# A block with product-key experts: 64 more tokens get their gates by accumulating transfers instead of one-hot matmuls

## The chip, the cores and the metric

The kernel runs on one core of a Trainium2 chip. The metric is the device time of one execution in microseconds (us). TensorE (PE) does the matmuls, VectorE (DVE) and ScalarE (ACT) the elementwise work, GpSimd (POOL) issues the indexed transfers, SyncE (SP) the plain ones.

## The reference

Two transformer layers follow each other; each ends in an expert layer ("peer"). Only the expert layer matters here. For 256 tokens, 8 heads and two halves per head, 128 scores are computed; the best 16 of each half are taken, their 256 sums are formed, the best 16 sums are taken, and each names one of 128 x 128 experts:

```python
top_s, top_i = lax.top_k(s, PEER_TOPK)
cand_s = top_s[..., 0, :, None] + top_s[..., 1, None, :]
cand_i = top_i[..., 0, :, None] * PEER_NKEYS + top_i[..., 1, None, :]
best_s, best_pos = lax.top_k(cand_s.reshape(...), PEER_TOPK)
idx = jnp.take_along_axis(cand_i.reshape(...), best_pos, axis=-1)
gate = jax.nn.softmax(best_s, axis=-1)
act = jax.nn.gelu(jnp.einsum('bpd,bphkd->bphk', hb, u))
out = jnp.einsum('bphk,bphkd->bpd', act * gb, v_tab[ib])
```

So each token has 8 x 16 = 128 picks, each an expert and a gate.

## The kernel before

The kernel doesn't gather experts. It computes all 16,384 experts for all 256 tokens: activations in `arena` (expert row i on the free axis, 128 columns per partition), then multiplies them by a matrix of gates that is zero where an expert was not picked, and then multiplies by the second table. An expert layer b (1 or 2) has these stages, in order of time:

1. `wq` and scores: the queries, and the 16 x 128 scores of each token in `s_area`.
2. u stage: 128 units of the first table, each 512 KB, stream through `ring` (four slots). ACT rounds a half unit (L1390), DVE takes the rest (L1393), PE does 24 matmuls a unit (L1315 to L1317), ACT takes the gelu (L1414). Between two half units DVE does one slot of other work, by the function `between`: in `topk_part` the ranking of one head of 128 tokens (10 slots), in `lookup_part` the finding of the experts and gates of 4 such items (18 slots). The slots are counted: 4 rounds of 4 items and one lookup make 4 x 58 = 232 slots of the 256 half units. Rounds 0 and 1 are the 8 heads of tokens 0 to 127, rounds 2 and 3 those of tokens 128 to 255.
3. Gates of tokens 0 to 127: after lookups 0 and 1 (`picks_ready`), POOL issues in `pool_scatter` 128 indexed transfers a layer (L1532), one for each head and rank. Each adds 128 words, one for each token, to a matrix in DRAM, `gates_dram`, that SP has filled with zeros early in the kernel (`zero_part`, 32 transfers in all, L1546). Two transfers may name the same cell, so the 16 transfers of a head wait until those of all heads before have landed (semaphore `scattered`).
4. Gates of tokens 128 to 255: PE turns the picks (`pe_turn`), then a one-hot stage makes 16 groups (`NG`) of 8 tokens: DVE and ACT write one-hot rows (`dve_hots` L1559 to L1564, `act_hots` L1573 and L1577), PE multiplies them (L1589), DVE multiplies the activations by the result (`dve_multiply`, L1598).
5. v stage: 128 units of the second table. SP first waits for `scattered` of the whole layer, then loads the gate rows from DRAM into `gring` (L1782), four ahead. DVE multiplies tokens 0 to 127 of an expert row by them (`multiply`, L1608), ACT and DVE split the product and the table (L1630, L1631, L1635, L1638), PE accumulates the output in all eight banks (L1321, L1322).

POOL does nothing else in the whole kernel.

Of the kernel before, what the change touches and what calls it, by code (L numbers as in the profile page):

```python
# [56 lines left out]
ZEROS = 512  # L57
NPROJ = 3
# [99 lines left out]
CONSTS = [("ident", 128), ("blk64", 128), ("iota", 128), ("token", 64)]  # L158
# [37 lines left out]
def shape_constants():  # L196

    i = np.arange(P)
    f32 = np.float32
    common = {  # L200
        "ident": np.eye(P), "blk64": i[:, None] // 64 == i[None, :] // 64,
        "iota": np.tile(np.arange(P), (P, 1)), "token": np.tile(i[:, None], (1, 64)),
    }
# [48 lines left out]
def build(nc, stream, xT, ctxT, metaT, vectors, common, consts1, consts2, keys1, keys2, w_a2, out):  # L252
# [35 lines left out]
    gring, _ = place("gring", [P, GATE_RING, P])  # L288
# [31 lines left out]
    gates_dram = {b: nc.dram_tensor(f"gates{b}", (P, P, P), F32, kind="Internal").ap() for b in (1, 2)}  # L320
# [115 lines left out]
    picks_best, gates = K.take(4, 64), K.take(4, 64)  # L436
    pos_f, rank1, rank2 = K.take(64), K.take(64), K.take(64)
    key_f, chosen = K.take(2, 64), K.take(2, 2 * 64)
    gate_sum = K.take(2, 4)
    K.at = (K.at + 7) // 8 * 8  # L440
    picks_pos, _ = place("picks_pos", [P, 64], U32, at=gbuf_at + K.at)
    picks_key, _ = place("picks_key", [P, 2, 64], U32, at=gbuf_at + K.at + 64)
    picks_at, _ = place("picks_at", [P, 2, 64], U32, at=gbuf_at + K.at + 192)
    K.take(320)
    hit = s_area[:, 0:64 * TOPK].rearrange("p (c a) -> p c a", a=TOPK)
    KINDS = 5
    sel = s_area[:, 1024:1024 + KINDS * P].rearrange("p (c t) -> p c t", c=KINDS)
# [878 lines left out]
    ITEMS = 4  # L1326
    ROUNDS = NT * HEADS // ITEMS
    ITEM_SLOTS, LOOK_SLOTS = 10, 18
# [87 lines left out]
    def topk_part(eng, i, q, n):  # L1416

        t, h = i // 2, (i % 2) * ITEMS + q
# [4 lines left out]
        best = picks_best[:, i, :]  # L1423
# [33 lines left out]
    def lookup_part(eng, b, i, n):  # L1457

        best = picks_best[:, i, :].rearrange("p (m k) -> p m k", k=TOPK)
        g4 = gates[:, i, :].rearrange("p (m k) -> p m k", k=TOPK)  # L1460
        row = slice(i % 2 * 64, i % 2 * 64 + 64)
        if n == 0:
            eng.tensor_copy(pos_f, picks_pos[:, :])
            eng.tensor_copy(key_f, picks_key[:, :, :])
            eng.tensor_tensor(g4, best, best[:, :, 0:1].broadcast_to([P, ITEMS, TOPK]), ALU.subtract)\
# [5 lines left out]
        if n == 2:  # L1471
            eng.scalar_tensor_tensor(rank2, rank1, -float(TOPK), pos_f, ALU.mult, ALU.add)
        if 3 <= n < 15:
            x, half, step = (n - 3) // 6, (n - 3) // 3 % 2, (n - 3) % 3
            c = slice(half * 32, half * 32 + 32)
            if step == 0:
                rank = (rank1, rank2)[x][:, c].rearrange("p (r o) -> p r o", o=1).broadcast_to([P, 32, TOPK])
                every = iota[:, 0:TOPK].rearrange("p (o a) -> p o a", o=1).broadcast_to([P, 32, TOPK])
                eng.tensor_tensor(hit[:, c, :], rank, every, ALU.is_equal)
            if step == 1:  # L1480
                keys = key_f[:, x, c].rearrange("p (h o a) -> p h o a", h=2, o=1).broadcast_to([P, 2, TOPK, TOPK])
                h4 = hit[:, c, :].rearrange("p (h k) a -> p h k a", h=2)
                eng.tensor_tensor(h4, h4, keys, ALU.mult)
            if step == 2:
                eng.tensor_reduce(chosen[:, x, row][:, c], hit[:, c, :], AX_X, ALU.add)
        if n == 15:
            eng.wait_ge(S("gates_exp"), ROUNDS * (b - 1) + i + 1)
            eng.tensor_reduce(gate_sum[:, 0, :], g4, AX_X, ALU.add)
            if i < 2:
                eng.scalar_tensor_tensor(chosen[:, 0, row], chosen[:, 1, row], float(P), chosen[:, 0, row],  # L1490
                                         ALU.mult, ALU.add)
        if n == 16:
# [3 lines left out]
        if n == 17:
            z = gate_sum[:, 1, :].rearrange("p (m o) -> p m o", o=1).broadcast_to([P, ITEMS, TOPK])
            ins = eng.tensor_tensor(g4, g4, z, ALU.mult)
            if i < 2:
                eng.tensor_copy(picks_at[:, i, :], chosen[:, 0, row])  # L1500
                eng.drain().then_inc(S("picks_ready"), 1)  # L1501
            if i == ROUNDS - 1:
                ins.then_inc(S("experts_chosen"), 1)
        eng.drain()

    def take_turned(dve, b):

        dve.wait_ge(S("experts_turned"), b)
        dve.tensor_copy(sel[:, 0:3, :], ps[:, 4, 0:3 * P].rearrange("p (c t) -> p c t", c=3))
        dve.tensor_scalar(sel[:, 3:5, :], ps[:, 4, P:3 * P].rearrange("p (c t) -> p c t", c=2), -1.0, None, ALU.mult)\  # L1510
           .then_inc(S("sel_taken"), 1)

    def pe_turn(pe, b):

        pe.wait_ge(S("experts_chosen"), b)
        late = gates[:, 2:4, :].rearrange("p a b -> p (a b)")
        for c, rows in enumerate((chosen[:, 0, :], chosen[:, 1, :], late)):
# [3 lines left out]
    def pool_scatter(pool, b):  # L1521
# [18 lines left out]
    PER_ZERO = P * P // ZEROS // ZERO_PARTS  # L1540
# [8 lines left out]
    NG = P // 8  # L1549
# [53 lines left out]
    def multiply(dve, b, i, s):  # L1603
# [3 lines left out]
        c = ds(i * (UB * T) + s * T, P)  # L1607
# [77 lines left out]
    def peer_act(act, b):  # L1685
# [78 lines left out]
    with nc.Block() as block:  # L1764
        @block.sync
        def _(sp):
# [18 lines left out]
            def peer_loads(b):  # L1785
# [14 lines left out]
                sp.wait_ge(S("scattered"), 16 * b * HEADS * TOPK)  # L1800
# [209 lines left out]
```

## Time and profile before

| | before |
|---|---|
| median of 3 runs | 2532.55 us (2528.1 to 2536.94) |
| the profiled execution's own time | 2529.04 us |
| its span | 2527.1 us |
| PE / DVE / ACT / POOL busy | 93% / 64% / 48% / 17% |
| granted TensorE clock | 0.973 |

The span runs from the first to the last instruction. A POOL transfer's busy time is the time that POOL takes to make it, not the time in which it lands. Idle time of an engine counts only where the end of the kernel waits for it.

### The profile page before, as it was taken

Reading aid. Unit: us, or ns where it says so; the run is one execution under the profiler, and the core shown is the slowest. Engines: PE = TensorE matmul, PEld = TensorE weight load, DVE = VectorE, ACT = ScalarE, POOL = GpSimd, SP = SyncE. Lnnn points to the kernel's source line nnn. Section 1 sums busy time; section 2 is a strip of 40 time slices with the busy share of each in tenths; the row PEclk is TensorE's granted clock in tenths of the full one; section 3 lists DMA queues with packets and bytes.
Section 4 is the critical chain, followed back from the end, with each engine's and each line's share of the span. In section 5 each row is a group of like instructions: output and inputs, shape, how many; then the busy total and the mean of one; then the engine's idle time right before and its main releaser. Section 6 shows DMA issues by size and latency. Waiting matters only on the chain.

```text
span 2527.1 us, 47068 instructions
## 1 busy us (share of the span) xinstructions
PE 2357.0 (93%) x14990; PEld 2098.7 (83%) x14990; DVE 1620.4 (64%) x3524; ACT 1216.9 (48%) x2578; POOL 424.0 (17%) x262
## 2 busy tenths in 40 slices
PE   7989979999997899999799899989999997899998
PEld 2767779999996788888668677779999996788887
DVE  2465345887877777777215674345887878777776
ACT  1356135555557555555223522035555557555554
POOL 0000000267763000000000000000277673000000
PEclk9989989999999999999899899989999999999999
DMA  6566443577762466665243322444577672466664
GB/s 234 175 225 217 158 150 141 183 183 183 182 184 55 155 210 206 211 209 203 102 142 117 100 89 96 142 153 147 183 181 181 185 180 52 159 214 211 211 214 166
DMA packets 190936, 422.57 MB, mean 167 GB/s; under 512 B 54256, under 2 KB 89328, under 8 KB 190208
## 3 DMA queue, kind: packets, MB, share of 16 engines
q1 hardware_dynamic: 149824, 413.73, 48.2%
q0 software_dynamic: 36864, 0.15, 4.3%
q10 hardware_dynamic: 4160, 7.64, 0.9%
q8 instruction: 40, 0.66, 0.1%
q14 instruction: 48, 0.39, 0.1%
HBM read 403.48 MB, written 17.96 MB: 167 GB/s over the span
## 4 chain that ended last, share of the span: by engine, by line
PE 87%; DVE 7%; issue 3%; ACT 2%; ACTq 0%; DMA 0%; DVEq 0%; PEld 0%; PEldq 0%
PE ps L714 20%; PE ps L1321 19%; PE ps L1315 11%; PE ps L1316 11%; PE ps L1317 11%; PE ps L1322 10%; PE ps L796 2%; DVE arena L1598 1%; DVE gbuf L1564 1%; PE ps L1007 1%; PE ps L985 1%; PE ps L1589 1%; PE ps L1353 1%; DVE gbuf L808 0%; PE ps L999 0%
## 5 line engine op out<-in xcount | busy, mean ns | idle before, releaser
L1321 PE MATMUL ps<-csplit,hl 128*128 128x512 f32 x2048 | 720.9, 397 | 7.0 <-DVE hl L1638 7.0
L1532 POOL DMA_INDIRECT gates<-gbuf,picks_at x256 | 423.2, 1653 | 1686.5 <-DVEq L1501 1517.3
L1315 PE MATMUL ps<-hsplit,hl 128*128 128x256 f32 x2304 | 656.6, 285 | 31.8 <-DVE hl L1393 31.8
L1316 PE MATMUL ps<-hsplit,hl 128*128 128x256 f32 x2304 | 655.7, 285 | 0.0
L1317 PE MATMUL ps<-hsplit,hl 128*128 128x256 f32 x2304 | 655.6, 285 | 0.0
L1322 PE MATMUL ps<-csplit,hl 128*128 128x256 f32 x2048 | 576.3, 281 | 0.0
L1393 DVE TENSOR_TENSOR hl<-ring,hl 128x512 fp32r<-128x512 f32 x576 | 399.1, 694 | 236.7 <-ACT hl L1390 225.7
L1390 ACT CAST hl<-ring 128x512 fp32r<-128x512 f32 x576 | 355.3, 620 | 371.6 <-PE ps L1317 370.9
L1315 PEld LDWEIGHTS ps<-hsplit,hl 128*128 128x128 f32 x2304 | 446.2, 194 | 32.9 <-ACT hl L1390 32.9
L1321 PEld LDWEIGHTS ps<-csplit,hl 128*128 128x128 f32 x2048 | 385.9, 188 | 97.8 <-issue 7.3
L714 PE MATMUL ps<-arena,ring 128*128 128x256 f32 (+2 forms) x1896 | 444.8, 394 | 15.5 <-issue 10.8
L1316 PEld LDWEIGHTS ps<-hsplit,hl 128*128 128x128 f32 x2304 | 446.2, 194 | 0.0
L1317 PEld LDWEIGHTS ps<-hsplit,hl 128*128 128x128 f32 x2304 | 446.0, 194 | 0.0
L714 PEld LDWEIGHTS ps<-arena,ring 128*128 128x128 f32 x1896 | 367.7, 196 | 77.6 <-issue 25.5
L1638 DVE TENSOR_TENSOR hl<-ring,hl 128x512 fp32r<-128x512 f32 x512 | 354.3, 693 | 75.8 <-ACT hl L1631 62.8
L1322 PEld LDWEIGHTS ps<-csplit,hl 128*128 128x128 f32 x2048 | 389.2, 190 | 0.0
L1631 ACT CAST hl<-ring 128x512 fp32r<-128x512 f32 x512 | 316.6, 619 | 80.7 <-PE ps L1322 80.7
L1630 ACT CAST csplit<-arena 128x256 fp32r (+1 forms) x256 | 104.3, 407 | 245.7 <-DVE arena L1608 233.3
L1635 DVE TENSOR_TENSOR csplit<-arena,csplit 128x256 fp32r<-128x256 f32 x256 | 108.9, 425 | 128.3 <-ACT csplit L1630 128.3
L1414 ACT ACTIVATE arena<-ps 128x256 f32<-128x256 f32 (+1 forms) x288 | 108.6, 377 | 18.0 <-PE ps L1317 17.9
L1589 PE MATMUL ps<-gbuf 128*128 128x128 f32 x512 | 68.1, 289 | 44.9 <-ACT gbuf L1577 25.5
L806 DVE TENSOR_SCALAR gbuf<-ps 128x256 f32<-128x256 f32 (+2 forms) x32 | 14.0, 437 | 141.7 <-PE ps L796 141.6
(196 smaller groups left out, 1830.4 us busy)
## 6 DMA issues: line engine op xcount, KB each, us to landing
ring<-stream SPq DMA_DIRECT2D x723, 512.0 KB
gates<-zeros SPq DMA_DIRECT2D x32, 512.0 KB, 5.0
gring<-gates SPq DMA_DIRECT2D x256, 64.0 KB, 2.9
gates<-gbuf,picks_at POOLq DMA_INDIRECT x256
arena<-keys ACTq DMA_DIRECT2D x2, 1024.0 KB, 4.9
gbuf<-consts ACTq DMA_DIRECT2D x1, 1120.0 KB, 5.0
arena<-xT ACTq DMA_DIRECT2D x1, 1024.0 KB, 10.6
arena<-ctxT ACTq DMA_DIRECT2D x1, 1024.0 KB, 12.9
```

Source lines behind the costliest of these rows:

```text
L714: mm = pe.matmul(ps[0:t.rows, t.bank, 0:t.cols], lhs, rhs, start=(t.start and i == 0), stop=(t.stop and i == last))
L1315: pe.matmul(out_ap, w[0], m[0], start=start, stop=False)
L1316: pe.matmul(out_ap, w[1], m[0], start=False, stop=False)
L1317: return pe.matmul(out_ap, w[0], m[1], start=False, stop=stop)
L1321: pe.matmul(ps[:, bank, :], w_hi, m_both, start=start, stop=False)
L1322: return pe.matmul(ps[:, bank, 0:T], w_lo, m_both[:, 0, :], start=False, stop=stop)
L1390: eng.copy(hl[:, hslot, 0, :], raw).then_inc(S("split_hi"), 1)
L1393: eng.tensor_tensor(hl[:, hslot, 1, :], raw, hl[:, hslot, 0, :].bitcast(F32), ALU.subtract)\
L1532: pool.indirect_dma_start(out=cells, out_offset=bass.IndirectOffsetOnAxis(ap=picks_at[:, i, c:c + 1], axis=0), in_=gates[:, i, c:c + 1], i ...
L1631: eng.copy(hl[:, hslot, 0, :], slot(unit)[:, part]).then_inc(S("split_hi"), 1)
L1635: eng.tensor_tensor(csplit[:, cslot, 1, :], acts[:, c], csplit[:, cslot, 0, :].bitcast(F32), ALU.subtract)
L1638: eng.tensor_tensor(hl[:, hslot, 1, :], slot(unit)[:, part], hl[:, hslot, 0, :].bitcast(F32), ALU.subtract).then_inc(S("split_lo"), 1)
```

## The change

Tokens 0 to 191 get their gates by transfers, and tokens 192 to 255 by the one-hot stage. The ranking goes head by head for both halves of the tokens (2 items and a lookup of 10 slots make a round, 8 rounds). After each lookup POOL issues for each of the 16 ranks one transfer of 128 words (tokens 0 to 127) and one of 64 words (tokens 128 to 191), each kind with a semaphore of its own. The matrix in DRAM has 192 columns instead of 128. The one-hot stage makes 8 groups instead of 16. The scratch tile `hit` lies in `gring` now.

```diff
+EXTRA = 64
+SENT = P + EXTRA
-    gring, _ = place("gring", [P, GATE_RING, P])
+    gring, _ = place("gring", [P, GATE_RING, SENT])
-    gates_dram = {b: nc.dram_tensor(f"gates{b}", (P, P, P), F32, ...
+    gates_dram = {b: nc.dram_tensor(f"gates{b}", (P, P, SENT), F32, ...
...
-    hit = s_area[:, 0:64 * TOPK].rearrange("p (c a) -> p c a", a=TOPK)
+    hit = gring[:, :, :].rearrange("p r c -> p (r c)")[:, 0:2 * TOPK * TOPK].rearrange("p (c a) -> p c a", a=TOPK)
+    STAGED = P - EXTRA
...
-    ITEMS = 4
-    ROUNDS = NT * HEADS // ITEMS
-    ITEM_SLOTS, LOOK_SLOTS = 10, 18
+    ITEMS = NT
+    ROUNDS = HEADS
+    ITEM_SLOTS, LOOK_SLOTS = 10, 10
...
-        t, h = i // 2, (i % 2) * ITEMS + q
+        t, h = q, i
...
+        if n == 9:
             eng.reciprocal(gate_sum[:, 1, :], gate_sum[:, 0, :])
...
+            eng.tensor_tensor(g2, g2, z, ALU.mult)
+            eng.tensor_copy(picks_at[:, i, :, :], cell)
+            eng.drain().then_inc(S("picks_ready"), 1)
...
-        pe.wait_ge(S("experts_chosen"), b)
+        pe.wait_ge(S("picks_ready"), ROUNDS * b)
...
-        for i in range(2):
-            pool.wait_ge(S("picks_ready"), 2 * (b - 1) + i + 1)
-            for head in range(ITEMS):
-                wait(pool, "scattered", 16 * sent)
+        for h in range(HEADS):
+            pool.wait_ge(S("picks_ready"), ROUNDS * (b - 1) + h + 1)
+            sent = ((b - 1) * HEADS + h) * TOPK
+            for t, n in enumerate((P, EXTRA)):
+                wait(pool, f"scattered{t}", 16 * sent)
                 for k in range(TOPK):
                     pool.indirect_dma_start(
...
+                        out=cells, out_offset=bass.IndirectOffsetOnAxis(ap=picks_at[0:n, h, t, k:k + 1], axis=0),
+                        in_=gates[0:n, t, h * TOPK + k:h * TOPK + k + 1], in_offset=None, compute_op=ALU.add,
+                        bounds_check=P * P * SENT - 1, oob_is_err=True).then_inc(S(f"scattered{t}"), 16)
...
-    PER_ZERO = P * P // ZEROS // ZERO_PARTS
+    PER_ZERO = P * SENT // ZEROS // ZERO_PARTS
-    NG = P // 8
+    NG = STAGED // 8
...
-        c = ds(i * (UB * T) + s * T, P)
+        c = ds(i * (UB * T) + s * T, SENT)
...
-                sp.wait_ge(S("scattered"), 16 * b * HEADS * TOPK)
+                for t in range(NT):
+                    sp.wait_ge(S(f"scattered{t}"), 16 * b * HEADS * TOPK)
```

On POOL, at the start of the first layer, these are the rows before; `scattered` is the landing of all transfers so far, `picks_ready` the end of a lookup:

```order
L1532 DMA gates<-gbuf,picks_at 2097152x1 [waits picks_ready,zeroed1]
L1532 DMA gates<-gbuf,picks_at 2097152x1 x15
L1532 DMA gates<-gbuf,picks_at 2097152x1 [waits scattered]
L1532 DMA gates<-gbuf,picks_at 2097152x1 x15
L1532 DMA gates<-gbuf,picks_at 2097152x1 [waits scattered]
L1532 DMA gates<-gbuf,picks_at 2097152x1 x15
L1532 DMA gates<-gbuf,picks_at 2097152x1 [waits scattered]
L1532 DMA gates<-gbuf,picks_at 2097152x1 x15
L1532 DMA gates<-gbuf,picks_at 2097152x1 [waits scattered,picks_ready]
L1532 DMA gates<-gbuf,picks_at 2097152x1 x15
```

And these are the rows now, `scattered0` for the transfers of 128 words and `scattered1` for those of 64:

```order
L1529 DMA gates<-gbuf,picks_at 3145728x1 [waits picks_ready,zeroed1]
L1529 DMA gates<-gbuf,picks_at 3145728x1 x31
L1529 DMA gates<-gbuf,picks_at 3145728x1 [waits scattered0,picks_ready]
L1529 DMA gates<-gbuf,picks_at 3145728x1 x15
L1529 DMA gates<-gbuf,picks_at 3145728x1 [waits scattered1]
L1529 DMA gates<-gbuf,picks_at 3145728x1 x15
L1529 DMA gates<-gbuf,picks_at 3145728x1 [waits scattered0,picks_ready]
L1529 DMA gates<-gbuf,picks_at 3145728x1 x15
L1529 DMA gates<-gbuf,picks_at 3145728x1 [waits scattered1]
L1529 DMA gates<-gbuf,picks_at 3145728x1 x15
```

A head has 32 transfers instead of 16, 256 a layer instead of 128, and each waits for those of its own kind of the head before, so 16 of the other kind stand between.

On SP, between the u stage and the v stage, this stood before:

```order
L1791 COMPARE_AND_BRANCH
L1771 DMA ring<-stream 128x1024 [waits split_lo] x4
L1782 DMA gring<-gates 128x128 [waits scattered]
L1782 DMA gring<-gates 128x128 x3
L1804 UNCONDITIONAL_BRANCH
```

And this stands there now:

```order
L1788 COMPARE_AND_BRANCH
L1768 DMA ring<-stream 128x1024 [waits split_lo] x4
L1779 DMA gring<-gates 128x192 [waits scattered1,scattered0]
L1779 DMA gring<-gates 128x192 x3
L1802 UNCONDITIONAL_BRANCH
```

The place is the same: four units of the second table are loaded, and then the queue waits until every transfer of the layer has landed.

## Rows read from the trace of the kernel before

**Rows 1.** The page: busy time by engine, and the queue of POOL's transfers.
```profile
PE 2357.0 (93%) x14990; PEld 2098.7 (83%) x14990; DVE 1620.4 (64%) x3524; ACT 1216.9 (48%) x2578; POOL 424.0 (17%) x262
...
q0 software_dynamic: 36864, 0.15, 4.3%
```
**Rows 2.** Windows: zeroing, then u stage, one-hot stage, v stage of both layers.
```profile
core 0: us, PE busy (x) PEld busy (x) DVE busy (x) ACT busy (x) POOL busy (x), PEclk, DMA share, GB/s
85.00:280.00 195.00, 172.94 (x780) 132.27 (x779) 118.48 (x204) 107.32 (x341) 0.00 (x0) 0.92 0.61 208
...
405.00:777.00 372.00, 370.65 (x3075) 370.52 (x3075) 286.30 (x748) 204.85 (x395) 205.52 (x125) 1.00 0.67 181
777.00:834.50 57.50, 33.97 (x257) 31.24 (x256) 55.74 (x112) 46.87 (x129) 4.95 (x4) 0.97 0.04 5
834.50:1198.00 363.50, 361.06 (x2036) 313.16 (x2037) 256.86 (x514) 198.09 (x384) 0.00 (x0) 1.00 0.61 206
1728.50:2102.00 373.50, 370.45 (x3075) 370.28 (x3075) 286.16 (x748) 206.44 (x398) 206.16 (x125) 1.00 0.66 180
```
**Rows 3.** Chain of waits, 777 to 840 us: start us, us, what.
```profile
788.38 1.13 DVE arena L1598
...
791.90 1.13 DVE arena L1598
...
833.49 1.23 DVE arena L1598
834.75 0.30 DVE arena L1608
835.46 0.62 ACT hl L1631
836.11 0.70 DVE hl L1638
836.94 0.77 PE ps L1321
```
**Rows 4.** POOL in order of time, first layer: start us, us, instruction, [idle before].
```profile
488.50 1.75 POOL L1532 DMA_INDIRECT gates<-gbuf,picks_at  x1 [487.08 <-DVEq L1501]
...
515.69 1.75 POOL L1532 DMA_INDIRECT gates<-gbuf,picks_at  x1 [0.30 <-issue]
520.09 1.74 POOL L1532 DMA_INDIRECT gates<-gbuf,picks_at  x1 [2.65 <-issue]
524.40 1.68 POOL L1532 DMA_INDIRECT gates<-gbuf,picks_at  x1 [2.57 <-DMA gates<-gbuf,picks_at]
...
549.36 1.54 POOL L1532 DMA_INDIRECT gates<-gbuf,picks_at  x1 [2.30 <-issue]
...
555.04 1.56 POOL L1532 DMA_INDIRECT gates<-gbuf,picks_at  x1 [2.29 <-issue]
...
781.29 1.57 POOL L1532 DMA_INDIRECT gates<-gbuf,picks_at  x1 [0.30 <-issue]
```
**Rows 5.** Line 1532 in 488 to 783 us: durations, then idle before it by cause.
```profile
L1532 POOL DMA_INDIRECT gates<-gbuf,picks_at x128: 1541/1547/2052, 488.5 to 781.3; - x128
...
  issue: 65.8, 121
  DMA gates<-gbuf,picks_at: 18.1, 6
```
**Rows 6.** In order of time: two lookups' last step, and SP's first gate loads.
```profile
487.27 0.19 DVE L1500 CAST picks_at<-gbuf 128x64 uint32<-128x64 f32 x1
...
570.79 0.19 DVE L1500 CAST picks_at<-gbuf 128x64 uint32<-128x64 f32 x1
...
784.32 1.75 SPq L1782 DMA_DIRECT2D gring<-gates  x4
```
**Rows 7.** Tile gates, 480 to 800 us: its loads by SP, and their landing.
```profile
L1782 SPq DMA_DIRECT2D gring<-gates x4: 328/432/433, 784.3 to 785.6; - x4
...
DMA to landing us min/median/max: 1.8/1.9/2.0
```
**Rows 8.** Groups by line in 405 to 777 us: count | busy us, mean ns | idle before.
```profile
L1479 DVE TENSOR_TENSOR s_area<-gbuf,con 128x512 f32<-128x512 f32 x16 | 11.0, 685 | 0.0
...
L1498 DVE TENSOR_TENSOR gbuf<-gbuf 128x64 f32<-128x64 f32 x4 | 0.9, 219 | 0.0
...
L1703 ACT ACT_TABLE_LOAD x4 | 5.1, 1283 | 0.1
```

More of the change, by code:

```diff
@@ L157 @@
         ("conv_w", 12), ("sink", 8), ("cond", 16)]
-CONSTS = [("ident", 128), ("blk64", 128), ("iota", 128), ("token", 64)]
+CONSTS = [("ident", 128), ("blk64", 128), ("iota", 128), ("token", 2 * TOPK)]
 CONSTS1 = [("rot", 128), ("cos", 256), ("sin", 256), ("mask", 1024)]
@@ L201, in shape_constants @@
         "ident": np.eye(P), "blk64": i[:, None] // 64 == i[None, :] // 64,
-        "iota": np.tile(np.arange(P), (P, 1)), "token": np.tile(i[:, None], (1, 64)),
+        "iota": np.tile(np.arange(P), (P, 1)), "token": i[:, None] + P * (np.arange(2 * TOPK)[None, :] // TOPK),
     }
@@ L318, in take @@
             return ap
-    gates_dram = {b: nc.dram_tensor(f"gates{b}", (P, P, P), F32, kind="Internal").ap() for b in (1, 2)}
+    gates_dram = {b: nc.dram_tensor(f"gates{b}", (P, P, SENT), F32, kind="Internal").ap() for b in (1, 2)}
     ps = nc.alloc_psum_tensor("ps", [P, 8, 512], F32)
@@ L435, in build @@
     K.take(8192)
[L436 to L439, printed above, removed]
-    K.at = (K.at + 7) // 8 * 8
[L441 to L444, printed above, removed]
-    hit = s_area[:, 0:64 * TOPK].rearrange("p (c a) -> p c a", a=TOPK)
+    picks_best, gates = K.take(NT, TOPK), K.take(NT, P)
+    pos_f, rank1, rank2 = K.take(2 * TOPK), K.take(2 * TOPK), K.take(2 * TOPK)
+    key_f, chosen = K.take(2, 2 * TOPK), K.take(2, NT, P)
+    cell_f = K.take(NT, TOPK)
+    gate_sum = K.take(2, NT)
+    K.at = (K.at + 7) // 8 * 8
+    picks_pos, _ = place("picks_pos", [P, 2 * TOPK], U32, at=gbuf_at + K.at)
+    picks_key, _ = place("picks_key", [P, 2, 2 * TOPK], U32, at=gbuf_at + K.at + 32)
+    picks_at, _ = place("picks_at", [P, HEADS, NT, TOPK], U32, at=gbuf_at + K.at + 96)
+    K.take(352)
+    hit = gring[:, :, :].rearrange("p r c -> p (r c)")[:, 0:2 * TOPK * TOPK].rearrange("p (c a) -> p c a", a=TOPK)
     KINDS = 5
-    sel = s_area[:, 1024:1024 + KINDS * P].rearrange("p (c t) -> p c t", c=KINDS)
+    STAGED = P - EXTRA
+    sel = s_area[:, 1024:1024 + KINDS * STAGED].rearrange("p (c t) -> p c t", c=KINDS)
     hot1 = gbuf[:, 0:GRING * 8 * P].rearrange("p (r t i) -> p r t i", r=GRING, t=8)
@@ L1422, in topk_part @@
         both = [(x, scores[:, x * P:(x + 1) * P], tmpbuf[:, x * P:(x + 1) * P]) for x in range(2)]
-        best = picks_best[:, i, :]
+        best = picks_best.rearrange("p t k -> p (t k)")
         if n == 0:
@@ L1457, in lookup_part @@
     def lookup_part(eng, b, i, n):
-        best = picks_best[:, i, :].rearrange("p (m k) -> p m k", k=TOPK)
-        g4 = gates[:, i, :].rearrange("p (m k) -> p m k", k=TOPK)
-        row = slice(i % 2 * 64, i % 2 * 64 + 64)
+        row = slice(i * TOPK, (i + 1) * TOPK)
+        g2, cell = gates[:, :, row], cell_f[:, :, :]
+        ranks = (rank1, rank2)
         if n == 0:
@@ L1464, in lookup_part @@
             eng.tensor_copy(key_f, picks_key[:, :, :])
-            eng.tensor_tensor(g4, best, best[:, :, 0:1].broadcast_to([P, ITEMS, TOPK]), ALU.subtract)\
+            eng.tensor_tensor(g2, picks_best, picks_best[:, :, 0:1].broadcast_to([P, NT, TOPK]), ALU.subtract)\
                .then_inc(S("gates_shifted"), 1)
@@ L1470, in lookup_part @@
             eng.tensor_scalar(rank1, rank1, ROUND, ROUND, ALU.add, ALU.subtract)
-        if n == 2:
+            eng.drain()
             eng.scalar_tensor_tensor(rank2, rank1, -float(TOPK), pos_f, ALU.mult, ALU.add)
-        if 3 <= n < 15:
-            x, half, step = (n - 3) // 6, (n - 3) // 3 % 2, (n - 3) % 3
-            c = slice(half * 32, half * 32 + 32)
+        if 2 <= n < 8:
+            x, step = divmod(n - 2, 3)
             if step == 0:
-                rank = (rank1, rank2)[x][:, c].rearrange("p (r o) -> p r o", o=1).broadcast_to([P, 32, TOPK])
-                every = iota[:, 0:TOPK].rearrange("p (o a) -> p o a", o=1).broadcast_to([P, 32, TOPK])
-                eng.tensor_tensor(hit[:, c, :], rank, every, ALU.is_equal)
+                rank = ranks[x].rearrange("p (r o) -> p r o", o=1).broadcast_to([P, 2 * TOPK, TOPK])
+                every = iota[:, 0:TOPK].rearrange("p (o a) -> p o a", o=1).broadcast_to([P, 2 * TOPK, TOPK])
+                eng.tensor_tensor(hit, rank, every, ALU.is_equal)
@@ L1480, in lookup_part @@
             if step == 1:
-                keys = key_f[:, x, c].rearrange("p (h o a) -> p h o a", h=2, o=1).broadcast_to([P, 2, TOPK, TOPK])
-                h4 = hit[:, c, :].rearrange("p (h k) a -> p h k a", h=2)
+                keys = key_f[:, x, :].rearrange("p (t o a) -> p t o a", t=NT, o=1).broadcast_to([P, NT, TOPK, TOPK])
+                h4 = hit.rearrange("p (t k) a -> p t k a", t=NT)
                 eng.tensor_tensor(h4, h4, keys, ALU.mult)
             if step == 2:
-                eng.tensor_reduce(chosen[:, x, row][:, c], hit[:, c, :], AX_X, ALU.add)
@@ L1486, in lookup_part @@
-        if n == 15:
+                eng.tensor_reduce(chosen[:, x, :, row], hit.rearrange("p (t k) a -> p t k a", t=NT), AX_X, ALU.add)
+        if n == 8:
             eng.wait_ge(S("gates_exp"), ROUNDS * (b - 1) + i + 1)
[L1488 to L1492, printed above, removed]
-            eng.reciprocal(gate_sum[:, 1, :], gate_sum[:, 0, :])
-            if i < 2:
-                eng.scalar_tensor_tensor(chosen[:, 0, row], chosen[:, 0, row], float(P), c_("token"), ALU.mult, ALU.add)
@@ L1496, in lookup_part @@
[L1496 to L1503, printed above, removed]
+            eng.tensor_reduce(gate_sum[:, 0, :], g2, AX_X, ALU.add)
+            eng.scalar_tensor_tensor(cell, chosen[:, 1, :, row], float(P), chosen[:, 0, :, row], ALU.mult, ALU.add)
@@ new lines, in lookup_part @@
+        if n == 9:
+            eng.reciprocal(gate_sum[:, 1, :], gate_sum[:, 0, :])
+            eng.scalar_tensor_tensor(cell, cell, float(SENT), c_("token").rearrange("p (t k) -> p t k", t=NT),
+                                     ALU.mult, ALU.add)
+            eng.drain()
+            z = gate_sum[:, 1, :].rearrange("p (m o) -> p m o", o=1).broadcast_to([P, NT, TOPK])
+            eng.tensor_tensor(g2, g2, z, ALU.mult)
+            eng.tensor_copy(picks_at[:, i, :, :], cell)
+            eng.drain().then_inc(S("picks_ready"), 1)
@@ L1508, in take_turned @@
         dve.wait_ge(S("experts_turned"), b)
-        dve.tensor_copy(sel[:, 0:3, :], ps[:, 4, 0:3 * P].rearrange("p (c t) -> p c t", c=3))
-        dve.tensor_scalar(sel[:, 3:5, :], ps[:, 4, P:3 * P].rearrange("p (c t) -> p c t", c=2), -1.0, None, ALU.mult)\
+        turned = ps[:, 4, 0:3 * P].rearrange("p (c t) -> p c t", c=3)[:, :, EXTRA:P]
+        dve.tensor_copy(sel[:, 0:3, :], turned)
+        dve.tensor_scalar(sel[:, 3:5, :], turned[:, 1:3, :], -1.0, None, ALU.mult)\
            .then_inc(S("sel_taken"), 1)
     def pe_turn(pe, b):
-        pe.wait_ge(S("experts_chosen"), b)
-        late = gates[:, 2:4, :].rearrange("p a b -> p (a b)")
-        for c, rows in enumerate((chosen[:, 0, :], chosen[:, 1, :], late)):
+        pe.wait_ge(S("picks_ready"), ROUNDS * b)
+        for c, rows in enumerate((chosen[:, 0, 1, :], chosen[:, 1, 1, :], gates[:, 1, :])):
             mm = pe.transpose(ps[:, 4, c * P:(c + 1) * P], rows, ident)
@@ L1595, in dve_multiply @@
         dve.wait_ge(S("e_ready"), g + (base(b) + GRING + 1))
-        a8 = acts[:, :].rearrange("p (i t) -> p i t", t=T)[:, :, ds(g * 8 + P, 8)]
+        a8 = acts[:, :].rearrange("p (i t) -> p i t", t=T)[:, :, ds(g * 8 + SENT, 8)]
         src = e_banks(slot_).rearrange("p (t i) -> p i t", t=8)
@@ L1702, in peer_act @@
                 act.wait_ge(S("gates_shifted"), ROUNDS * (b - 1) + i + 1)
-                act.activation(gates[:, i, :], gates[:, i, :], ACT.Exp).then_inc(S("gates_exp"), 1)
+                row = gates[:, :, i * TOPK:(i + 1) * TOPK]
+                act.activation(row, row, ACT.Exp).then_inc(S("gates_exp"), 1)
         take_unit(act, b, N_IT, -2)
```

6 lines of the change are left out of this document (removed).

## The prediction

> **What bounds the kernel now.** I read the page first, then the stages by windows, then the chain of waits between the stages, then POOL in order of time.
>
> [...] The one-hot stage is different: PE is busy 33.97 of 57.5 us, DVE 55.74, and DVE sets the pace [rows 2]. Two multiplies L1598 start 3.52 us apart (788.38, 791.90), which is what a group costs [rows 3]. After the last one the v stage's PE start (836.94) comes 2.19 us behind the first multiply L1608 (834.75) [rows 3].
>
> POOL looks idle (17% over the span, [rows 1]), but not where it works. From 488.50 to 781.29 + 1.57 = 782.86 us it makes 128 transfers [rows 4, 5]: 294.4 us. It works 205.52 + 4.95 = 210.5 us of them [rows 2], 1.644 us a transfer. The other 83.9 us (65.8 + 18.1, [rows 5]) are 127 intervals: the ordinary one is 0.30 us, and 18 are 1.97 to 3.76 us long, so the long ones hold 83.9 - 127 x 0.30 = 45.8 us above the ordinary. SP loads the first gates at 784.32 [rows 6], 1.46 us behind POOL's last instruction. The one-hot stage runs until 834.7, so today POOL ends with 50 us to spare, which is what hides it. The question is what doubles there.
>
> **The change, part by part.**
>
> One-hot stage: 8 groups fewer, 8 x 3.52 = 28.2 us a layer, 56.3 us in all. The first and last groups keep their own costs. By this alone v would start at 836.94 - 28.2 = 808.8 us.
>
> When POOL may start: the two lookups end 58 slots apart, 570.79 - 487.27 = 83.52 us [rows 6], so a slot is 1.440 us. The first lookup ends with slot 30 instead of slot 58: 28 x 1.440 = 40.3 us sooner, and POOL starts at 488.50 - 40.3 = 448.2. The last lookup (slot 240) lets its head go at 448.2 + 210 x 1.44 = 750.6; only 32 transfers stand behind it, so it doesn't decide if POOL is behind by then.
>
> What POOL has to do: 128 transfers of 128 words at 1.644 + 0.30 = 1.944 us, 248.8 us as before. Then 128 of 64 words, for which no row exists. Nearest row: 1.644 us for 128 words. From below, the whole of it is made word by word and half the words take 0.822. From above, it is a fixed price and takes 1.644. A price below proportion has no reason in the rows. I take the middle, 1.233 us (an estimate), since one size can't divide a fixed part from one by the word; with 0.30 between, 128 x 1.533 = 196.2 us.
>
> The long intervals: their places are regular. In the first layer one stands before transfers 15, 30, 45 and so on to 120 (8 times: 520.09, 555.04 and on), one before each head (6 marked as DMA waits: 524.40 is number 16), and one before 28, 56, 84 (549.36 is number 28) [rows 4]. Those at the heads are the semaphore's, and they go: 16 transfers of the other kind now stand between. Those at every 15th and 28th need something filled by a count of entries. [...] They cost 2.62 - 0.30 = 2.32 us each (mean of the 11 that stand at no head), 46.4 us. So the stops don't go with the semaphores; their number stays near what it was.
>
> Sum for POOL: 248.8 + 196.2 + 46.4 = 491.4 us. Less 7 us: once DVE is idle a transfer takes the least, 1.541 instead of 1.644 [rows 5], and some 38 pairs fall there. It ends at 448.2 + 484.4 = 932.6. Then 1.46 us to SP, 0.43 us issue, 1.9 us landing [rows 7] (96 KB instead of 64, +0.1), and 2.1 us through multiply, split and first matmul [rows 3]: PE starts v at about 938.6 instead of 836.94, 101.7 us later. The one-hot stage and its gain lie wholly inside. The second layer has the same counts and the same stage lengths [rows 2]: twice, +203.4 us.
>
> [...]
>
> The rest:
> - DVE in the u stage: 48 hit steps of 512 elements as before (0.685 us, [rows 8]). The small steps of a lookup (about 0.2 us, [rows 8]) come 8 times instead of 4, some 12 a lookup: +10 us. DVE idles 372 - 286 = 86 us there [rows 2]. Cost nothing. Without that cover, at most the 10 us a layer.
> - ACT: 4 more exponentials, each with two table loads of 1.283 us [rows 8], +11 us against 167 us idle [rows 2], in pieces of 2.8 us that two split units hold. Nothing.
> - DVE in the v stage: the multiply grows from 128 to 192 columns, at most half of 0.30 us more a unit, 19 us against 363.5 - 256.9 = 107 us idle [rows 2, 3]. Nothing.
> - Zeroing: 768 KB a part instead of 512; at the 208 GB/s of that stretch 16 x 256 KB would be 20 us of transfer a layer, but the engines are busy for 0.61 and PE misses only 22 of 195 us [rows 2]. Between 0 and 10 us; I take 1.
>
> Against the profiled execution: 2529.0 + 203.4 + 1 = 2733.4 us. The median of the runs is 3.5 us above that execution, inside their spread of 9 us, so I give 2734.
>
> **The rivals.**
>
> Same price for half the words (1.644). For it: the durations cluster at 1541 to 1547 ns [rows 5], as a fixed routine would; the shape of the words shows nowhere. POOL ends 128 x 0.411 = 52.6 us later a layer: 2734 + 105 = 2839 us. Against it: 128 addresses have to be read and written in some way. [...]
>
> The landing sets the pace, not POOL: 144 packets in 294.4 / 128 = 2.30 us before, 144 + 80 = 224 now, 3.58 us a pair. 128 x 3.58 = 458 us, v starts at 912, 75 us late a layer: 2680. Against it: outside the counted stops POOL goes on after 0.30 us each time.
>
> The transfers stay hidden and the kernel is faster. PE must start v before 836.94, so POOL must end by 831: 382.8 us, less 248.8 and 46.4, leaves 87.6 us for 128 small ones, 0.38 us each beside the interval. That is under a quarter of 1.644. Should they be as cheap as 0.2 us, the end of POOL is at 807.5 and PE starts v at 813.5, 23 us earlier a layer: 2482 us; the floor is 2529 - 56 = 2473. For it: only that no row shows a small one, and that my count of stops is a guess (without any stop the point is 0.75 us, still less than half).
>
> That the change fails to move the tokens is excluded: `NG` counts 8, and POOL has 256 rows a layer.
>
> **How the numbers follow.** A price between half and nine tenths of 1.644: 0.62. Same price: 0.21. Landing: 0.06. Hidden: 0.11, nearly all of it faster, for the band of no change (0.3%, 7.6 us, about what can be told from none) is only 0.03 us of price wide on either side. Faster 0.09, same 0.02, slower 0.89. The ends: price 0.822 gives 52.6 us less a layer, 2629; price 1.644 gives 2839. With the uncertainty of the stops, 2615 to 2850. It leaves out the hidden case.
>
> **What would show it.** Right: on POOL two lengths of transfer in turns, no idle over 1 us at heads, stops at counts of about 10 and 18 pairs, a first start near 448, the last near 930. PE idle for some 130 us between L1589 and L1321, released through L1608 by the gate loads. Groups of the one-hot stage still 3.5 us apart, ending near 806. Wrong: POOL done before 831, or small transfers under 0.4 us, or PE with gaps in the u stage.

## The result and the profile after

| | before | after |
|---|---|---|
| median | 2530.32 us (4 runs) | 2757.21 us (4 runs, 2752.91 to 2758.33) |
| profiled execution, span | 2527.1 us | 2756.3 us |
| ratio to before | | 1.0886, 95% interval 1.0862 to 1.0910 |

The change costs 227 us; the forecast was 2734 (2615 to 2850).

The page of the changed kernel, busy time by engine and the queue of POOL's transfers, beside [rows 1]:

```profile
PE 2327.1 (84%) x14734; PEld 2068.0 (75%) x14734; DVE 1594.1 (58%) x3520; ACT 1191.3 (43%) x2474; POOL 800.1 (29%) x518
...
q0 software_dynamic: 57344, 0.23, 6.5%
```

PE works 30 us less (256 one-hot matmuls fewer) and POOL 376 us more. 57344 packets for 512 transfers are 112 each, the mean of 144 (36864 for 256 before, [rows 1]) and 80: a 64-word transfer takes 80, the number that the forecast has for it in the rival of the landing.

The stages of the first layer by windows (columns as in [rows 2]):

```profile
405.00:777.00 372.00, 368.42 (x3060) 368.25 (x3059) 292.13 (x802) 217.87 (x411) 261.28 (x165) 1.00 0.69 180
777.00:810.00 33.00, 21.18 (x158) 19.59 (x156) 28.05 (x56) 23.85 (x66) 26.22 (x16) 0.95 0.24 16
810.00:953.00 143.00, 0.00 (x0) 0.00 (x0) 1.44 (x5) 1.20 (x3) 111.89 (x76) 0.51 0.19 3
953.00:1317.00 364.00, 361.84 (x2064) 315.40 (x2064) 270.52 (x526) 200.55 (x391) 0.00 (x0) 0.99 0.68 221
```

The u stage is as full as before (PE 368.42 us of 372, 370.65 before [rows 2]); the one-hot stage is over at 810 instead of 834.7. Then come 143 us in which only POOL works, 111.89 us of them, and the granted clock falls from 1.00 in the u stage to 0.51 while PE waits. The second layer shows the same from 2241 to 2384.

The chain of waits at the end of this gap (start us, us, what), where [rows 3] stood before:

```profile
944.83 1.41 POOL gates L1529
946.25 0.31 issue
946.55 2.71 DMA gates<-gbuf,picks_at
...
949.33 1.91 DMA gring<-gates
...
951.33 0.37 DVE arena L1604
...
951.80 0.40 ACT csplit L1626
952.21 0.53 ACT hl L1627
...
952.76 0.70 DVE hl L1634
...
953.60 0.76 PE ps L1325
```

Before, the v stage was released by the last multiply of the one-hot stage (L1598); now by the last of POOL's transfers, its landing (2.71 us, its making included), the load of the gates and the multiply. The same gap in the list of waits, both layers (engine, line, waited for: us in total, times, longest):

```profile
PE ps L1325 <- DVE hl L1634: 288.0, 2, 144.8
DVE arena L1604 <- DMA gring<-gates: 280.9, 2, 141.3
```

PE's first v matmul is at 953.60 instead of 836.94. From the first query matmul of a layer (L1319, L1315 before) to its first v matmul (L1325, L1321 before) it is:

| | before | after | later |
|---|---|---|---|
| layer 1 | 346.0 to 836.9 | 349.4 to 953.6 | 113.3 us |
| layer 2 | 1671.4 to 2161.8 | 1781.1 to 2384.6 | 113.1 us |

226.4 of the 229.2 us of span lie there. The other 2.8 are made of 3.4 more ahead of the first layer, 5.4 less and 6.4 more in the two v stages, and 1.6 less between the layers. No run ties them to the change: the v stage has two lengths in the kernel before too (last section), and the start of the first layer moves by some us from execution to execution (see "The zeroing").

### The profile page after: what moved, and what is told of

The parts are those of the page before. It is cut to its first block, busy times and chain, and to the rows that moved or that the text cites. A ratio compares the mean times of both kernels' runs of the same rounds, so it can differ in the third digit from the quotient of the medians.

```text
span 2756.3 us, 46894 instructions
## 1 busy us (share of the span) xinstructions
PE 2327.1 (84%) x14734; PEld 2068.0 (75%) x14734; DVE 1594.1 (58%) x3520; ACT 1191.3 (43%) x2474; POOL 800.1 (29%) x518
## 3 DMA queue, kind: packets, MB, share of 16 engines
q0 software_dynamic: 57344, 0.23, 6.5%
## 4 chain that ended last, share of the span: by engine, by line
PE 43%; POOL 11%; issue 7%; DVE 3%; ACT 1%; DMA 0%; POOLq 0%; DVEq 0%; ACTq 0%; SPq 0%
PE ps L1325 17%; POOL gates L1529 11%; PE ps L718 10%; PE ps L1326 9%; PE ps L1319 2%; PE ps L1320 1%; PE ps L1321 1%; PE ps L800 1%; PE ps L989 0%; DVE gbuf L812 0%; PE ps L1247 0%; PE ps L1357 0%; PE ps L1011 0%; DVE arena L1196 0%; DVE arena L1209 0%
## 5 line engine op out<-in xcount | busy, mean ns | idle before, releaser
L1529 POOL DMA_INDIRECT gates<-gbuf,picks_at x512 | 799.2, 1561 | 1578.2 <-issue 1127.1
L1325 PE MATMUL ps<-csplit,hl 128*128 128x512 f32 x2048 | 721.9, 398 | 288.0 <-DVE hl L1634 288.0
L1319 PE MATMUL ps<-hsplit,hl 128*128 128x256 f32 x2304 | 656.8, 285 | 31.8 <-DVE hl L1397 31.8
L1325 PEld LDWEIGHTS ps<-csplit,hl 128*128 128x128 f32 x2048 | 387.0, 189 | 381.9 <-issue 288.3
L1321 PE MATMUL ps<-hsplit,hl 128*128 128x256 f32 x2304 | 655.9, 285 | 0.0
L1319 PEld LDWEIGHTS ps<-hsplit,hl 128*128 128x128 f32 x2304 | 446.6, 194 | 32.9 <-ACT hl L1394 32.9
L1321 PEld LDWEIGHTS ps<-hsplit,hl 128*128 128x128 f32 x2304 | 446.6, 194 | 0.0
L1634 DVE TENSOR_TENSOR hl<-ring,hl 128x512 fp32r<-128x512 f32 x512 | 354.3, 693 | 76.8 <-ACT hl L1627 64.1
L1604 DVE TENSOR_TENSOR arena<-arena,gring 128x192 f32 (+1 forms) x256 | 90.0, 352 | 281.1 <-DMA gring<-gates 280.9
```

Of the source, the lines that this page charges most:

```text
L1319: pe.matmul(out_ap, w[0], m[0], start=start, stop=False)
L1321: return pe.matmul(out_ap, w[0], m[1], start=False, stop=stop)
L1325: pe.matmul(ps[:, bank, :], w_hi, m_both, start=start, stop=False)
L1529: pool.indirect_dma_start(out=cells, out_offset=bass.IndirectOffsetOnAxis(ap=picks_at[0:n, h, t, k:k + 1], axis=0), in_=gates[0:n, t, h * ...
L1634: eng.tensor_tensor(hl[:, hslot, 1, :], slot(unit)[:, part], hl[:, hslot, 0, :].bitcast(F32), ALU.subtract).then_inc(S("split_lo"), 1)
```

## The experiments

Each is an edit of the changed kernel unless it says otherwise. For each, "POOL" is the time from its first to the end of its last transfer of the first layer, and a stop is an interval over 1 us between two transfers in which POOL doesn't wait for a ranking.

**The loss is the 64-word transfers**

```diff
-            for t, n in enumerate((P, EXTRA)):
+            for t, n in enumerate((P,)):
...
-                for t in range(NT):
-                    sp.wait_ge(S(f"scattered{t}"), 16 * b * HEADS * TOPK)
+                sp.wait_ge(S("scattered0"), 16 * b * HEADS * TOPK)
```

> The changed kernel without its 64-word transfers (the gates of tokens 128 to 191 stay zero, so their part of the expert layer is left out); everything else of the change stands. Theory (POOL's making of the 64-word transfers is the whole loss): POOL then has 16 transfers a head, 31 us against 43 us in which a head is ranked, ends near 790, and the one-hot stage of 8 groups (last matmul at 808.5) sets the start of the v stage near 812. Two layers give back 2 x 25 us against the kernel before: span near 2478, time 2480, faster than before by 2%. Rival (finer ranking, wider multiply, wider gate loads or zeroing cost more than a few us): 2510 or more, with idle PE in the u or v stage.

Measured: 2474.09 us, ratio 0.978 (0.9738 to 0.9822). POOL ends at 789.75, and PE starts v at 813.4. Its windows (columns as in [rows 2]):

```profile
405.00:777.00 372.00, 368.41 (x3052) 368.25 (x3052) 291.39 (x802) 218.03 (x411) 201.53 (x122) 0.99 0.68 180
777.00:813.00 36.00, 22.82 (x166) 21.64 (x164) 29.76 (x61) 25.30 (x70) 10.92 (x7) 0.91 0.17 26
813.00:1170.00 357.00, 356.65 (x2048) 311.72 (x2048) 265.62 (x515) 196.43 (x381) 0.00 (x0) 1.00 0.68 222
```

PE is as full in the u and v stages as before (368.41 of 372 us and 356.65 of 357). So the finer ranking, the wider multiply (352 instead of 285 ns, the median) and the wider loads cost nothing that can be seen. The shorter one-hot stage gives what was worked out for it: from the first query matmul to the first v matmul it is 462.5 us (350.9 to 813.4) instead of 490.9, 28.4 less. All the loss, and more, is the 128 transfers a layer that were taken out here.

**What a transfer costs by its words**

```diff
-            for t, n in enumerate((P, EXTRA)):
+            for t, n in enumerate((P, 32)):
```

> The changed kernel with 32 words instead of 64 in each transfer of the second kind (tokens 160 to 191 get no gates from transfers; that part is left out). Theory (a price per transfer, nearly without the words: 1.41 us for 64 words and 1.54 for 128 give 0.0021 us a word): least 1.34 us, mean near 1.41, POOL ends 8 us sooner a layer, time near 2740. Rival (proportional below 64 words): least 0.7 us, POOL 90 us sooner a layer, time under 2600.

> The same with 16 words (tokens 144 to 191 left out of the transfers). Theory of the price per transfer: least 1.31 us, time near 2732. Rival of the price by the word: least 0.35 us, the transfers hidden, time near 2480. [...]

Measured: 2741.16 us, as expected, and 2722.41 us where 2732 was expected (one run each). Of these 10 us, 7 lie in the second v stage, which took 356.5 us here and 363.9 in the changed kernel. From line 1529 of the three kernels in the first layer, after, 32 words and 16 words; the three numbers are least, median and greatest ns of all 256 transfers, half of them of 128 words:

```profile
L1529 POOL DMA_INDIRECT gates<-gbuf,picks_at x256: 1405/1546/2407, 452.2 to 946.6; - x128
```
```profile
L1529 POOL DMA_INDIRECT gates<-gbuf,picks_at x256: 1326/1546/2390, 451.7 to 937.1; - x128
```
```profile
L1529 POOL DMA_INDIRECT gates<-gbuf,picks_at x256: 1293/1546/2101, 452.0 to 934.3; - x128
```

| words | least us | mean us of the 128 in layer 1 |
|---|---|---|
| 128 | 1.541 | 1.643 |
| 64 | 1.405 | 1.476 |
| 32 | 1.326 | 1.404 |
| 16 | 1.293 | 1.357 |

The least times are 1.26 us and 0.0022 us a word: nearly all of the price is the transfer's, not the words'. An eighth of the words still costs 83% of the mean. The proportional rival is out.

**Where the stops come from**

The forecast had 20 stops a layer, the trace shows 8 in each layer, each before the 16th transfer of a head (483.89 is number 15, counted from 0). POOL in order of time, changed kernel:

```profile
479.88 1.55 POOL L1529 DMA_INDIRECT gates<-gbuf,picks_at  x1 [0.30 <-issue]
483.89 1.94 POOL L1529 DMA_INDIRECT gates<-gbuf,picks_at  x1 [2.46 <-issue]
```

```diff
+            wait(pool, "scattered", 16 * 2 * sent)
             for t, n in enumerate((P, EXTRA)):
-                wait(pool, f"scattered{t}", 16 * sent)
...
-                        bounds_check=P * P * SENT - 1, oob_is_err=True).then_inc(S(f"scattered{t}"), 16)
+                        bounds_check=P * P * SENT - 1, oob_is_err=True).then_inc(S("scattered"), 16)
...
-                for t in range(NT):
-                    sp.wait_ge(S(f"scattered{t}"), 16 * b * HEADS * TOPK)
+                sp.wait_ge(S("scattered"), 2 * 16 * b * HEADS * TOPK)
```

> The changed kernel with one semaphore for both kinds of transfers; a head's first transfer waits for all of the head before. [...] Rival (a stop belongs to the 16th transfer of a head, whatever the semaphore): 8 stops and 7 head waits, +15 us a layer, time near 2788.

Measured: 2837.93 us (one run), where 2840 was expected. POOL 534.2 us, 25 stops, where 27 were expected: 20 by count and 7 at heads. POOL in order of time, the start of the second head (number 32) and what follows:

```profile
522.07 1.56 POOL L1529 DMA_INDIRECT gates<-gbuf,picks_at  x1 [2.87 <-DMA gates<-gbuf,picks_at]
...
530.16 1.88 POOL L1529 DMA_INDIRECT gates<-gbuf,picks_at  x1 [2.73 <-issue]
...
537.08 1.95 POOL L1529 DMA_INDIRECT gates<-gbuf,picks_at  x1 [3.05 <-issue]
```

They stand at 15, 32, 35, 37, 55, 64, 70, 74, 96, 105, 111, 128, 133, 140, 151, 160, 170, 175, 192, 207, 212, 224, 229, 247, 250. The heads are 32, 64 and so on to 224. The other places follow from the two counts that the kernel before shows, whose stops stand at every 15th and at every 28th transfer of 128 words [rows 4], if one of 64 words counts as 0.53 of one of 128. The count up to 15, beginning anew at each of its stops, gives 15, 37, 55, 74, 96, 111, 133, 151, 170, 192, 207, 229, 247; the count up to 28 gives 35, 70, 105, 140, 175, 212, 250. Together with the heads these are the 25 places, none missing and none over (96 and 192 are heads too). The second layer is a check, because the counts run on from the first: they give 23 places there (10, 32, 47, 64, 67, 69 and on to 244), and the trace has exactly these 23. The 0.53 is an estimate, fitted to the 48 places (anything from 0.525 to 0.545 gives them); the packets stand as 80 to 144, 0.56. What is counted, and where it is kept, no trace shows. So the stops come by count, as the forecast had them; what was missing is that with a second semaphore only 8 a layer are left, of the 25 and 23.

```diff
-            for t, n in enumerate((P, EXTRA)):
-                wait(pool, f"scattered{t}", 16 * sent)
-                for k in range(TOPK):
+            for part, t, n in ((0, 0, P), (0, 1, EXTRA), (1, 0, P), (1, 1, EXTRA)):
+                if part == 0:
+                    wait(pool, f"scattered{t}", 16 * sent)
+                for k in range(part * 8, part * 8 + 8):
```

> The changed kernel with each head's transfers in another order: 8 of 128 words, 8 of 64, 8 of 128, 8 of 64, on the same two semaphores. Theory (stops come only where a run on one semaphore is longer than 15 transfers of 128 words): no interval over 1 us is left on POOL, 18.7 us less a layer, time near 2720. Rival (stops come by a count of entries, whatever the run): 8 stops or more stay and the time stays at 2757.

Measured: 2728.02 us, ratio to before 1.0778 (1.073 to 1.0826), 29 us under the change where 37 were expected. No stop is left in either layer. The causes of idle time before line 1530, first layer (us, times):

```profile
  DVEq L1501: 449.5, 1
  issue: 77.4, 254
  DMA gates<-gbuf,picks_at: 0.3, 1
```

255 intervals are 77.7 us, 0.305 each: only the ordinary one. POOL is 480.7 instead of 495.7 us: 18.7 us of stops less, but the 64-word transfers took 1.50 us on average instead of 1.48, which is 3.5 us a layer and most of what is missing from the 37. So the stop belonged to the length of the run (transfers in a row on one semaphore), not to the 16th rank.

The kernel before with half the `dynamic_dma_scratch_size`:

```diff
-    nc = bacc.Bacc("TRN2", target_bir_lowering=False, num_devices=1, dynamic_dma_scratch_size=4096)
+    nc = bacc.Bacc("TRN2", target_bir_lowering=False, num_devices=1, dynamic_dma_scratch_size=2048)
```

> [...]

Measured: 2539.86 us (one run, before 2534.1 beside it). In both layers the stops now stand, as expected, at every 7th transfer, at the heads, and nowhere else; POOL in order of time, numbers 6, 7, 13 and 14:

```profile
504.51 1.55 POOL L1532 DMA_INDIRECT gates<-gbuf,picks_at  x1 [0.30 <-issue]
509.23 1.56 POOL L1532 DMA_INDIRECT gates<-gbuf,picks_at  x1 [3.18 <-issue]
...
520.76 1.55 POOL L1532 DMA_INDIRECT gates<-gbuf,picks_at  x1 [0.30 <-issue]
524.94 1.54 POOL L1532 DMA_INDIRECT gates<-gbuf,picks_at  x1 [2.64 <-issue]
```

POOL takes 314.4 instead of 294.4 us (some 15 more were expected) and ends at 806.9, still under the one-hot stage. The kernel before doesn't feel it: from the first query matmul to the first v matmul it is 490.8 us (350.2 to 841.0), as before. In the changed kernel nothing covers POOL's end, and there a stop costs time, as the two edits above show.

**The zeroing**

In the kernel before, zeroing transfers of 768 KB over a padded matrix of gates:

```diff
+    gates_wide = {b: nc.dram_tensor(f"gates{b}", (P, 48, 512), F32, kind="Internal").ap() for b in (1, 2)}
...
-        rows = gates_dram[b].rearrange("j i t -> j (i t)")[:, n * PER_ZERO * ZEROS:(n + 1) * PER_ZERO * ZEROS]
+        rows = gates_wide[b].rearrange("j a c -> j (a c)")[:, n * 3 * ZEROS:(n + 1) * 3 * ZEROS]
...
```

> The kernel before with zeroing transfers of 768 KB instead of 512 KB (the gate matrix padded to half as much again, gates where they were within it). Theory (the larger zeroing delays all before the first expert layer): the first matmul of the query stage starts at 349.4 instead of 346.0, the time grows by 3 to 5 us. Rival (scatter of the first stages): it starts at 346 again.

Measured: 2529.14 us (one run). The first query matmul starts at 355.0, later than in the changed kernel, and yet the whole isn't longer. With the narrow zeroing of before it started at 346.0 and, in the kernel with half the scratch size, at 350.2; with the wide one between 348.6 and 353.0 in the five edits of the changed kernel above. A cost of some us ahead of the first layer is neither shown nor excluded. The opposite edit, narrow transfers in the changed kernel, leaves a third of the matrix without a value and gave no time.

**A version that follows from it: packed transfers**

If the price is the transfer's, 64 words waste half of one. Two ranks of one head never name the same expert for a token, so they may share a transfer. ACT's queue copies cells and gates of the extra tokens into all 128 partitions, and POOL makes 8 transfers for 16 ranks:

```diff
+                for j in range(FOLD):
+                    to, k = slice(j * EXTRA, (j + 1) * EXTRA), j * PACK
+                    act.dma_start(pack_at[to, h, :], picks_at[0:EXTRA, h, 1, k:k + PACK]).then_inc(S(f"packed{h}"), 16)
+                    act.dma_start(pack_gate[to, h, :], gates[0:EXTRA, 1, h * TOPK + k:h * TOPK + k + PACK])\
+                       .then_inc(S(f"packed{h}"), 16)
...
+                        out=cells, out_offset=bass.IndirectOffsetOnAxis(ap=pack_at[:, h, k:k + 1], axis=0),
+                        in_=pack_gate[:, h, k:k + 1], in_offset=None, compute_op=ALU.add,
```

> The changed kernel with the same 64 extra tokens, but two ranks of a head share one transfer of 128 words: after each lookup ACT's queue copies the cells and gates of tokens 128 to 191 into all 128 partitions (four small transfers), and POOL makes 8 transfers for them a head instead of 16, in runs of 8 (8 of tokens 0 to 127, 4 packed, and again). Theory (POOL's time is the number of transfers, 1.95 us each with the interval): 24 a head, 192 a layer, 374 us, so from 452 to 826, PE starts the v stage at 832 instead of 837: 10 us less in all than the kernel before, time 2520 (ratio 0.996). Rival (the words are what costs): as slow as the change, 2757. Second rival (copies on ACT's queue delay ACT or the picks): gaps of PE in the u stage and a time above before.

Measured: 2520.98 us, ratio 0.9961 (0.9940 to 0.9982). POOL 378.4 us for 192 transfers without a stop, to 830.95, and PE starts v at 836.7 instead of 832: POOL's transfers were 1.67 us each, not the 1.65 that the expectation has, and landing, load and splits behind the last one take 5.7 us, as in the changed kernel. Same words, same tokens, a quarter fewer transfers than the change: 236 us less. 29 of them are the stops, as the runs of 8 showed; the other 207 go with the fewer transfers.

The same with 32 extra tokens and four ranks a transfer (`EXTRA = 32`, so 32 tokens fewer in the one-hot stage than before, 12 groups instead of 16; 20 transfers a head):

> The same with 32 extra tokens and four ranks in one transfer: 4 packed transfers a head, 20 in all, 12 groups of 8 tokens in the one-hot stage, gate matrix 160 wide. Theory: 20 x 1.95 = 39 us a head is less than the 43 us in which a head is ranked, so POOL ends near 797, the one-hot stage (4 groups x 3.52 = 14.1 us shorter) sets the v stage's start near 823 to 826; 2 x 14 us less than before and up to 3 us more for the zeroing: time near 2504, ratio 0.990, faster than both kernels. Rival (the copies get in the way, or the start of the v stage is held by something else): not below 2525.

Measured: 2522.15 us, ratio 0.9948 (0.9929 to 0.9968): faster than before, but by some 9 us and not by the 27 that were expected. The rival's cause, the copies in the way, is the right one, though the time lies just under its bound. From the first query matmul to the last of the u stage it is 439.1 us (349.7 to 788.8) instead of 430.5 before. ACT in order of time, in the first of the eight heads, shows why:

```profile
457.38 0.62 ACT L1399 CAST hl<-ring 128x512 fp32r<-128x512 f32 x1 [0.76 <-PE ps L1326]
457.39 0.64 ACTq L1721 DMA_DIRECT2D pack_at<-picks_at  x1
...
461.96 0.61 ACTq L1722 DMA_DIRECT2D gbuf<-gbuf  x1
462.67 1.14 ACT L1399 CAST hl<-ring 128x512 fp32r<-128x512 f32 x2 [4.39 <-PE ps L1326]
```

Eight issues of 0.60 to 0.67 us stand in a row, and the next split comes after 4.39 us of idle time, where 0.59 and 0.76 are usual; that it is more than the split halves in hand cover is inferred from PE's loss. (With four issues of 0.55 to 0.71 us in a row, in the packed version above, the stretch didn't grow: 430.1 us.) So the copies go two a unit over four units (and POOL's runs become 15, 2, 1, 2):

```diff
-        pack_now = {(i + 1) * ROUND_SLOTS // 2 + 2: i for i in range(ROUNDS)}
+        pack_now = {(i + 1) * ROUND_SLOTS // 2 + 2 + j: (i, j) for i in range(ROUNDS) for j in range(FOLD)}
```

> The packed kernel with 32 extra tokens, with the eight copies of a head issued two a unit over four units instead of all at once on ACT's queue, and POOL's runs 15, 2, 1, 2 instead of 8, 2, 8, 2. Theory (each issue holds ACT for 0.6 us, the burst of eight holds it 5.3 us, more than the split ring covers, and cost 8.6 us of PE a layer): two issues, 1.3 us, fit into ACT's idle time of 1.3 us a unit, the u stage is back at 430.5 us from the first query matmul to its last, PE starts the v stage near 827, and the time is near 2505, ratio 0.989 to before. Rival (the u stage is longer for another reason, such as the DMA engines' load): the u stage stays at 439 us and the time at 2522.

Measured: 2500.21 us, ratio 0.9869 (0.9839 to 0.9899). The stretch is 430.5 us again (349.9 to 780.4), PE starts v at 826.8, and the chain of waits there is the one-hot stage's, as in [rows 3], not POOL's:

```profile
821.25 2.04 PE ps L1599 x16
...
823.31 1.23 DVE arena L1608
...
824.57 0.34 DVE arena L1618
...
826.80 0.65 PE ps L1330
```

POOL is done at 796.2. This version is 31 us faster than the kernel before and 257 us faster than the change.

One thing in it sharpens the finding on the stops. Its runs hold 15 transfers, not 16, and yet all eight heads of both layers have a stop behind the run, before the first packed transfer. It isn't a wait for the copies. In the first head, shown here, the last of them was issued at 467.3:

```profile
480.06 1.55 POOL L1535 DMA_INDIRECT gates<-gbuf,picks_at  x1 [0.30 <-issue]
484.12 1.55 POOL L1543 DMA_INDIRECT gates<-gbuf,pack_at  x1 [2.51 <-issue]
```

So 15 in a row are already too many here, 16 times out of 16, and only runs of 8 were seen without a stop (0 in the 512 transfers of the runs-of-8 kernel, 0 in the 384 of the packed one). It costs nothing here, since POOL isn't the last to finish.

## Why the prediction was right

The mechanism came out as forecast: POOL is the bound between the u and the v stage, PE stands still there, the gain of the one-hot stage lies inside the gap, and PE is as full in the u and v stages as before. The time was nearer than the terms behind it, because two errors cancelled. The terms, layer 1:

| term | forecast us | measured us |
|---|---|---|
| query start to POOL's start, against before | -40.3 | 102.8 - 142.5 = -39.7 |
| 128 transfers of 128 words | 210.4 | 210.3 |
| 128 transfers of 64 words | 157.8 | 188.9 |
| stops above the ordinary interval | 46.4 (20) | 18.7 (8) |
| ordinary intervals | 76.8 | 77.8 |
| relief once DVE is idle | -7 | in the two rows of transfers |
| POOL from first to last | 484.4 | 495.7 |
| POOL's end to PE | 6.0 | 5.6 |
| v stage later | 101.7 | 113.3 |

The term mis-sized is the price of a 64-word transfer: I took three quarters of 1.644, 1.233 us, as the middle between two bounds. It is 1.476, 0.90 of the price of 128 words, at the very edge between the forecast and the rival "same price". The rival was the better picture of the price: the size test shows a fixed 1.26 us. The middle of two bounds was a choice without a row, 31 us a layer too low. What the words add is small, 0.25 us on 1.29 when 16 become 128, though it shows from the smallest step on (0.03 us from 16 to 32 words); POOL's time for a transfer as a whole, 1.29 us and more, sets the pace.

The stops went the other way, 28 us a layer too high, and by luck hid most of that error: 31.1 - 27.7 + 7 + 1 = 11.4 us a layer, which is the 113.3 against 101.7 but for 0.2. No run with two semaphores shows the 20 stops behind the 46.4 us, or stops at counts of about 10 and 18 pairs: the trace of the change has 8 a layer, one at each head. With one semaphore 20 come by count, 13 and 7 over the 128 pairs of the first layer. The 7 is the relief. It came (once DVE is idle a 128-word transfer took 1.55 us instead of 1.67, a 64-word one 1.41 instead of 1.51), but beside DVE the 128-word ones took 1.67 here where they had taken 1.64 before, so their mean stayed at 1.64. "The stops don't go with the semaphores" was wrong, although by count they come as forecast: without the second semaphore the time is 2838. Had only the price been right, the forecast would have been 2734 + 62 = 2796. Had only the stops been right, it would have been 2734 - 55 = 2679, and the rival "same price" 2839 - 55 = 2784, against 2757 measured.

The other rivals: landing does not set the pace. By that rival a pair of transfers takes 2.30 us for each 144 packets, so with 16 words (144 + 32 packets, from the 45056 that the queue shows for 512 transfers) it would take 2.81 us; it took 3.63 without the stops, and the runs-of-8 kernel has no interval but the ordinary one. Hidden transfers are out by the size test, since even 16 words cost 1.29 us where 0.38 was needed, or 0.75 without any stop. The zeroing (1 us) stays open, smaller than the scatter.

What a stop waits for, no trace shows; it is mostly 1.8 to 4 us long. What is shown is: on one semaphore stops fall by count, and on two in turns only where a run holds 15 transfers of 128 words or more (15 and 16 were tried, and 8 without a stop).

## What to carry to other kernels

Price indexed transfers from GpSimd by their number, not by their words (1.48 us for 64, 1.64 for 128), and fill each with as many rows as it takes before splitting work into more of them. An engine that is 17% busy over the span can be the next bound. What counts is how long it works between the point where its work may begin and the point where its result is needed: in the kernel before that was 294 us out of the 343 between 488.5 and 831. Before issuing more small copies from an engine's queue, look at how many may stand in a row there: behind eight of them ACT's next split waited 4.39 us. When neither bound of an unknown price has a row, say which one a mechanism speaks for before taking the middle.

## What the hardware showed unexpectedly

- A transfer of 16 words, added into DRAM, takes POOL 1.29 us at least, one of 128 words 1.54.
- On one semaphore POOL stops before every 15th and every 28th transfer of 128 words, for 2.0 to 3.8 us (kernel before, first layer: 18 stops with those at the heads), and with half the `dynamic_dma_scratch_size` before every 7th (24 stops). With two semaphores in turns there are 0 stops in the 256 transfers of a layer with runs of 8, but one in each head with runs of 15 or 16.
- Issuing a copy of half a KB from ACT's queue took ACT 0.5 to 0.7 us; eight in a row cost PE 8.6 us over a layer, or about 1.1 us each burst.
- POOL's making of a transfer is slower while DVE works: 1.67 against 1.55 us for 128 words, 1.51 against 1.41 for 64 (means of the first layer up to 808 us, and after it, where DVE is busy for 1.44 of 143 us).
- The v stage takes either 355 to 358 or 363 to 364 us from its first to its last matmul, whatever the kernel (before: 362.9 in layer 1, 357.5 in layer 2; after: 357.5 and 363.9). No experiment here touches the cause, and two such stages can move a single run by 13 us.
